# The two MLP products by seven half-block products in place of eight, sums on the vector engine

## The reference, cut to what matters

```python
h = h + mix                                   # after attention; 1024 tokens x 1024 channels
h = h + squared_relu_mlp(rms_norm(h, mlp_norm[i]), mlp_w_up[i], mlp_w_down[i])

def squared_relu_mlp(h, w_up, w_down):        # w_up 1024 x 4096, w_down 4096 x 1024
    a = jax.nn.relu(h @ w_up)
    return (a * a) @ w_down
```

## Time and profile before

| | us |
|---|---|
| median of three runs | 2296.77 |
| span of the profiled execution | 2296.6 |
| stage `so` | about 258 to 342 |
| MLP, first to last matmul | 343.15 to 1041.5 |
| final norm, first operand of the Fourier stage | to 1054 |

### The profile page before, as it was taken

How to read it: one execution, slowest core, us unless ns; L and a number is a source line. 1 busy time by engine, 2 the same in 40 slices (tenths; PEclk the granted TensorE clock), 3 DMA queues, 4 the chain that set the end, 5 groups by cost and what they waited for, 6 DMA issues and landing times.

```text
span 2296.6 us, 27818 instructions
## 1 busy us (share of the span) xinstructions
PE 2222.8 (97%) x11316; PEld 1856.7 (81%) x11316; DVE 1450.6 (63%) x2316; ACT 971.2 (42%) x1521; POOL 214.8 (9%) x316
## 2 busy tenths in 40 slices
PE   8999999999999999999999999999998999899997
PEld 6898788888888888887888898788887886688886
DVE  7777445465564555567623227378887754799996
ACT  6777422111111111134422224366766322478785
POOL 0011000011010010100000014000000100211211
PEclk9999999999999999999999999999999999899998
DMA  3123512242342343323122112000001612799996
GB/s 146 47 79 122 195 46 61 81 138 87 98 137 92 101 133 97 110 102 67 54 79 92 35 45 88 28 1 1 1 1 42 256 55 102 299 393 386 386 379 225
DMA packets 79872, 280.64 MB, mean 122 GB/s; under 512 B 9936, under 2 KB 10224, under 8 KB 78592
## 3 DMA queue, kind: packets, MB, share of 16 engines
q1 hardware_dynamic: 48960, 172.84, 21.1%
q0 software_dynamic: 29632, 101.83, 14.2%
...
HBM read 243.17 MB, written 35.66 MB: 121 GB/s over the span
## 4 chain that ended last, share of the span: by engine, by line
PE 86%; DVE 7%; ACT 4%; issue 1%; DMA 1%; POOLq 0%; SPq 0%; ACTq 0%; DVEq 0%
PE psum L98 26%; PE psum L100 25%; PE psum L99 25%; PE psum L2471 2%; PE psum L2482 2%; ACT MP_hi L2572 1%; PE psum L978 1%; DVE MP_lo L2665 1%; ACT PB L2538 1%; DVE small L2618 1%; PE psum L951 1%; PE psum L3309 1%; PE psum L3038 1%; DVE idx L3011 1%; DVE cur L3014 0%
## 5 line engine op out<-in xcount | busy, mean ns | idle before, releaser
L98 PE MATMUL psum<-U_hi,w_hi 128*128 128x512 f32 x688 | 271.0, 394 | 13.4 <-DVE w_lo L243 10.7
L234 ACT ACTIVATE w_hi<-raw 128x1024 fp32r<-128x1024 f32 (+2 forms) x163 | 162.7, 1002 | 280.5 <-PE psum L100 267.7
L99 PE MATMUL psum<-U_lo,w_hi 128*128 128x512 f32 x688 | 269.0, 391 | 0.0
L100 PE MATMUL psum<-U_hi,w_lo 128*128 128x512 f32 x688 | 268.7, 391 | 0.0
L243 DVE TENSOR_TENSOR w_lo<-raw,w_hi 128x1024 fp32r<-128x1024 f32 (+2 forms) x162 | 187.9, 1167 | 113.3 <-ACT w_hi L234 113.1
L98 PE MATMUL psum<-W_hi,w_hi 128*128 128x512 f32 x512 | 199.7, 390 | 0.9 <-DVE X L1092 0.9
L100 PE MATMUL psum<-W_hi,w_lo 128*128 128x512 f32 x512 | 199.2, 389 | 0.0
L99 PE MATMUL psum<-W_lo,w_hi 128*128 128x512 f32 x512 | 199.2, 389 | 0.0
L98 PE MATMUL psum<-a_hi,w_hi 128*128 128x512 f32 x512 | 199.2, 389 | 0.0
L99 PE MATMUL psum<-a_lo,w_hi 128*128 128x512 f32 x512 | 199.2, 389 | 0.0
L100 PE MATMUL psum<-a_hi,w_lo 128*128 128x512 f32 x512 | 199.2, 389 | 0.0
...
## 6 DMA issues: line engine op xcount, KB each, us to landing
rawe<-in_w_e SPq DMA_DIRECT2D x112, 512.0 KB, 16.9
mraw<-in_w_mod POOLq DMA_DIRECT2D x128, 256.0 KB, 3.0
rawx<-in_w_e SPq DMA_DIRECT2D x56, 512.0 KB, 18.0
raw<-in_w_up SPq DMA_DIRECT2D x32, 512.0 KB, 3.6
raw<-in_w_dn SPq DMA_DIRECT2D x32, 512.0 KB, 3.6
raw<-in_w_e SPq DMA_DIRECT2D x24, 512.0 KB, 17.0
X<-in_xT SPq DMA_DIRECT2D x8, 512.0 KB, 9.4
raw<-in_w_q SPq DMA_DIRECT2D x8, 512.0 KB, 4.9
```

What stands on the lines that cost most here:

```text
L98: e.matmul(o, l[0], r[0], start=first, stop=False, skip_group_check=skip)
L99: e.matmul(o, l[0], r[1], start=False, stop=False, skip_group_check=skip)
L100: return e.matmul(o, l[1], r[0], start=False, stop=last, skip_group_check=skip)
L234: act.e.activation(hi, src, ACT.Copy).then_inc(w_hi, 1)
```

## The change

Split both operands of a product in 2 x 2 blocks. The plain way takes eight block products; the change takes seven, with sums of blocks as operands and sums of products as results.

**First product (up).** The weight is cut into 16 groups of two column blocks (256 columns of w_up), with two halves of 512 input channels; the moving side into channel halves and token halves. Each group g is seven products of 4 x 3 matmuls, 84 in all, where two column blocks took 96. The seven moving operands B1 to B7 (four tiles of 128x512, high and low) are made once, in stage `so` and the first group, from X, in place; so X is saved to DRAM first (`x1r`) and comes back in the down stage. The form is one with few sums in which products 2, 7 and 3 are added in PSUM onto products 1, 6 and 5, after ACT has copied these out. For each group DVE makes four sums of weight halves (S1 to S4) and, from the products, the four results, their ReLU, and seven combinations t1, ..., t7 of the squared results, which SP stores to DRAM (`ta`), 256 KB each. ACT squares in place.

**Second product (down).** 7 passes of 8 steps; a step has 24 matmuls (4 output rows x 2 x 3), 1344 in all where 1536 were. A step needs three loads of 512 KB (two blocks of w_down and one of `ta`; in passes 3 and 4 of the form only one block of w_down), one DVE sum of the two blocks (passes 1, 2, 5, 6, 7), and two tiles to split. After each pass DVE adds its four results into one or two places of X (12 x 4 additions of 128x512). The weight ring has 12 raw buffers and 8 places here; splitting runs three steps ahead of PE, the sum four.

**Modulation.** 28 steps go with the groups of the up stage, 68 with steps 6 to 47 of the down stage (rows that serve both vectors are loaded once), 32 move to the later stage `gates_b`. In the first two, SP loads the rows, in the same queue as the weights.

```diff
@@ so_dve: operands of the up products, made in place
-            if 0 < n < 7:
-                u(n - 1)
-        u(6)
-        u(7)
+            if 0 < n < 5:
+                k = n - 1
+                copy_lo(dve, 1, k, X[:, k, half(0)])
+                dve.wait_ge(*so.dve("lo1", k))
+                e.tensor_tensor(X[:, k, half(0)], X[:, k, half(1)], X[:, k, half(0)], ALU.subtract).then_inc(
+                    *so.dve.one("sum5", k))
+            if 1 < n < 6:
+                copy_lo(dve, 5, n - 2, X[:, n - 2, half(0)])
+            if n > 4:
+                scaled_lo(dve, 3, n - 5, 1)
+                sum7(dve, n - 5)
+                sum6(dve, n - 5)
+        scaled_lo(dve, 3, 3, 1)
+        sum7(dve, 3)
+        for k in range(3):
+            copy_lo(dve, 7, k, X[:, k, half(1)])
         for i in range(2):
             nm2.add_half(dve, i)
-        for i in range(2):
-            nm2.inverse(dve, i)
+        copy_lo(dve, 7, 3, X[:, 3, half(1)])
+        for k in range(4):
+            scaled_lo(dve, 2, k, 0)
+        sum6(dve, 3)
@@ up_act, the head of each group
+            if g:
+                make_hi(act, T_U1[g])
+                square(g - 1, "a21", 0, "r21")
+                if g == 1:
+                    act.wait_ge(*srow_in.at(1))
+                    act.e.activation(srow[:], srow[:], ACT.Silu).then_inc(*ml.act.one("silu", 0))
+                p1(g)
+                p6(g)
+                p5(g)
@@ up_dve, one group (g > 0, not the last); up_ends(g-1) is c21, r21, lo, t6, t3, lo
+            if g:
+                up_ends(dve, g - 1)
+            else:
+                for k in range(4):
+                    copy_lo(dve, 6, k, X[:, 4 + k, half(1)])
+                make_lo(dve, T_U1[0])
...
+            if last:
+                down_sum(dve, 0)
+            else:
+                dve.wait_ge(*lo_mark(T_UY[g]))
+                weight_sums(dve, ml, g + 1)
+            if g:
+                up_last(dve, g - 1)
+            else:
+                make_lo(dve, T_U0[1])
+                for i in range(2):
+                    nm2.inverse(dve, i)
...
+            e.tensor_tensor(c[1][:], c[0][:], c[1][:], ALU.add).then_inc(*ml.dve.one("u", g))
...
+            relu(dve, c[3], bank(up_bank(g, 2)), 0, "r11", g)
...
+            e.tensor_tensor(rg[0][:], c[3][:], c[2][:], ALU.add).then_inc(*ml.dve.one("t1", g))
@@ up_pe
+        for g in range(N_G):
+            for i in THEN if g else FIRST:
+                b, (ts, h) = up_bank(g, i), OPERAND[i]
+                w = use(pe, ts[g])
+                if i in ONTO:
+                    pe.wait_ge(*ml.act(ONTO[i], g))
+                else:
+                    claim(pe, b)
+                for k in range(4):
+                    if g == 0:
+                        pe.wait_ge(*so.dve(f"lo{i}", k))
+                    m = mm3(pe.e, bank(b), cols([x[:, half(h)] for x in w], k, 128), ch(B_OP[i], k, 0, 512),
+                            k == 0 and i not in ONTO, k == 3, True)
+                m.then_inc(*ml.pe.one("u", g, i))
+                if (g, i) == (0, 5):
+                    for y in range(2):
+                        nm2.sums(pe, y)
@@ down_sp, down_dve, down_pe
+    def down_sp(sp):
+        for s in range(5, N_S):
+            down_raws(sp, s)
+            for r in down_rows(s):
+                if r > 3:
+                    sp.wait_ge(*ml.dve("mod", *row_jobs(r - 4)[-1]))
...
+                sp.e.dma_start(dmraw[r % 4][:], A["w_mod"][D_ROWS[r]]).then_inc(dmraw_in[r % 4].sem, 16)
...
+        for s in range(N_S):
+            make_lo(dve, make_ahead(s))
+            for y in evict_at(s):
+                evict(*y)
+            for r in down_rows(s):
...
+                    mod_step(dve, who, i, dmraw[r % 4], dsrow[who], to)
+            for y in squares_at(s - 1):
+                adds(*y)
+            if s + 4 < N_S:
+                down_sum(dve, s + 4)
...
+        for s in range(N_S - 2):
+            for d in range(4):
+                m = step(s, d, s % 8)
```

925 lines of the change are left out of this document (643 added, 282 removed).

## The result

The changed kernel takes 2253.43 us (median of four runs, 2251.31 to 2256.98) against 2296.36 of the kernel before on the same chip: a ratio of 0.9813, 95% interval 0.9801 to 0.9824. The prediction was 2232 with a range of 2219 to 2258. The direction was right and the time lies in the range, but the gain is 43 us where 65 were forecast. Of the 20.7 us that the spans lack, 17.7 lie in the down stage.

A forecast was written before the change was run, and what follows sets the result against it. PE was taken to bound the kernel, busy 97% of the span. Matmuls removed -87.1, up start +14.7, down stage +7, MLP end 0, gates_b modulation +0.5 sum to -64.9 from 2296.6: 2232 us, range 2219 to 2258.

The forecast's parts named there:

- The price of a matmul: In the MLP each matmul costs 0.2267 us of PE; 384 removed give -87.1 us.
- Rival 5: A matmul's price is its duration, 0.39 us, so 150 us less, 2170 us; chance 0.01.
- Steady up groups: Up groups in steady state: DVE's 17.1 us fit within PE's 19.0 per group; cost 0, hidden behind PE.
- The start: Start of the up stage: PE waits on the DVE and ACT chain to product 1's copy; +14.7 us, bounds +8 and +20.
- The down stage: Down steps: PE bounds on average, with some waits for DVE, ACT and loads; +7 us, bounds 0 and +32.
- The reserve: Down stage: DVE may fall 12.9 us behind before PE waits; steps 20 to 35 lose 14, about 2 us of waits.
- Steps 44 to 51: Down steps with additions of squares: some 13 us lost by DVE, about 0.5 us of cost.
- Steps 0 to 11: First down steps: only 2.5 us in hand, DMA also brings back X and stores; about 3 us of waits.
- Rival 1: Down stage bound by DVE or late loads by more: +10 to +30 us, 2242 to 2262; chance 0.24.
- Rival 2: Clock falls with small waits: about 6 down steps each bring a spell of 3 us, 18 us, 2250; chance 0.06.
- Rivals 3 and 4: 3: cheaper start, no down-stage waits, 2222, chance 0.16; 4: SP's modulation waits make loads late, 2420, chance 0.03.
- The end of the MLP: From last matmul through the norm's sums: 6 to 8 us against 7.3; 0, bounds -1.5 and +2.5.

The follow-up runs named there:

- the eighth product: Changed kernel with the 12 matmuls of product 4 done twice in each of the 16 up groups: 2293.7 us, ratio 0.9988 to the kernel before.
- rows later: Changed kernel with SP issuing each down-stage modulation row three iterations later, behind the weight loads of step s+3: 2247.1 us, ratio 0.9784 to the kernel before.
- short additions: Changed kernel with the 28 additions of squares for the final norm on 16 of 512 columns, part of the work left out: 2248.2 us, ratio 0.9789.
- sums first: Changed kernel with modulation rows issued three iterations later and DVE's sum of step s+4 right behind the low parts of step s+3: 2236.5 us, ratio 0.9742.
- X later: Changed kernel with X's reload spread behind down steps 2, 5, 8, 10 and first-pass results added in steps 12 to 15: 2252.3 us, ratio 0.9810.
- all: Kernel of by room, with X reloaded in pieces behind steps 2, 4, 6, 8 and first results added in steps 10 to 13: 2227.5 us, ratio 0.9698.
- by room: Kernel of three orders, with the down stage's modulation rows dealt out by DVE's load: 2234.2 us, ratio 0.9722 to the kernel before.
- three orders: Changed kernel with rows later, sums first, and the second up group's ACT copies ahead of all first-group squares, silu behind: 2233.3 us, ratio 0.9728.

## Why the prediction was right or wrong

**The price of a matmul** was right, by the eighth product in the up stage. Rival 5 (duration) is excluded.

**Steady up groups** were right: 17.1 us of DVE per group forecast, 17.15 measured (198.54 of 220 us, times 19.0), 972 matmuls per 220 us, and behind 384 us no wait of PE up to 696 us.

**The start** was right in size, +14.7 against +15.3, and in its steps: the wait ahead of the norm's sums 2.94 us (3 forecast), PE goes on behind the copy of product 1 of the second group at 383.44, 43.4 us behind the end of `so`'s last matmul (42.3 forecast), the wait there 8.48 (6 to 9 forecast), a lower clock behind it: the first matmul at 383.44 takes 0.79 us, and the silu's place in the chain is shown by its move. Of the 1.1 us too few, 0.9 is a slip of the sum: four low parts of B6 are 2.5 us at 0.62, and it went from 12.4 to 14.0 with them; DVE took 2.4 (352.84 to 355.26). Not foreseen was a third wait of 0.78 us at 361.

**The down stage** is the step that failed, +7 against +24.7. Of it 17.2 us are PE's nine waits. For 10.2 us the granted clock was at the lower level behind the two long ones, which is about 5 us at half the pace; the 2 to 3 us left were not traced. DVE's step was nearly right: 5.7 and 6.9 forecast, 5.84 and 7.04 measured (832.41 to 838.25, 863.54 to 870.58). Three sizes hung on it:
- *The reserve.* "12.9 in hand less 1 not yet regained" was not there at step 20, since SP's waits for modulation held back the loads of the passes without sums, in which it is won. The prediction named these waits but charged them only to steps with sums (1.5 us for all), and gave the steps 20 to 35 about 2 us; PE's three waits from 867 to 888 us are 4.0. Shown by rows later: 9.9 us, 1.2 of them in the two waits of the seam. My sign for it was wrong too: I looked for DVE's waits ended by DMA, of which there is nearly none from 709 us on; ACT's are the ones to look at.
- *Steps 44 to 51*, forecast 0.5. With four additions of squares in a step DVE took 8.25 us per step twice in a row (931.42 to 939.67 to 947.92), and PE's waits of 2.0 and 5.41 us and a lower clock follow. Shown by the short additions, 6.3 us of the down stage. With rows later and sums first they cost nothing, so this and the reserve are one loss seen twice, not two to be added.
- *Steps 0 to 11*, forecast 3 us, measured 5.3 of waits and the clock behind them (0.72 from 706 to 712). Here the loads were late by traffic: X's reload of 4.2 MB beside the weights. I had put "DMA has to bring back X" into the 3 us without a price. X later (3.5 us) and, within "all", 5.7 us of the stage show the size of it; that it is the reload and not the results moved along with it is read from DVE's wait of 5.02 for DMA, not shown by a run of its own.

Rival 1, DVE or late loads by 10 to 30 us, is thus what happened (17.7 above the term), and its time, 2242 to 2262, holds the measured one; its price and its mechanism were told. The range reached to 2258 for this rival's sake; that is why the time lies in it with a term off by 17.7, and no merit of the term. Its chance, 0.24, was held down by the argument that passes without sums give reserve back; that was true of DVE's work and not of the loads.

**Rival 2**, the clock with small waits. In 860 to 960 us PE paused four times by 1.3 to 2.0 us and the granted clock stayed at the upper level:

```profile
860.00:960.00 100.00, 93.58 (x406) 75.43 (x405) 84.24 (x135) 43.93 (x50) 0.54 (x1) 1.00 0.76 280
```

In the same trace it was at the lower level behind the waits of 2.94, 8.48, 4.00 and 5.41 us (0.72 in the window at 706; matmuls of 0.79 and 0.77 us at 383.44 and 980.74) and through the sums at the end of the MLP. So the rival did not come as written, one spell of 3 us behind each of some six small waits. But the length of a pause doesn't tell alone. With the rows later the clock fell behind one of 2.0 us,

```profile
699.52 0.52 PE L99 MATMUL psum<-w_hi 128*128 128x512 f32 x1 [2.04 <-DVE w_lo L281]
699.50:703.50 4.00, 3.98 (x11) 3.18 (x12) 0.00 (x0) 0.00 (x0) 0.00 (x0) 0.57 1.00 409
```

and with the short additions it stayed up behind one of 3.7 us:

```profile
709.04 0.47 PE L99 MATMUL psum<-w_hi 128*128 128x512 f32 x1 [3.67 <-DVE w_lo L281]
709.00:713.00 4.00, 3.96 (x18) 3.30 (x18) 2.87 (x3) 2.35 (x3) 0.00 (x0) 1.00 1.04 409
```

By the rule of the Trainium skill that the prediction weighed (TensorE: Matmul & The Clock Gate, "A second HAM failure mode: psum-queue depth-cycling") brief pauses between groups of matmuls would have made it swing. From 860 to 960 us this trace, as that of the experts before, does not agree for pauses up to 2.0 us; the two pauses of 2.0 us with the rows later agree with it.

**Rivals 3 and 4.** The cheaper start was not there; the down stage nearly without waits came only with the orders of "all", 22.5 us below the changed kernel's. SP's waits did make loads late, but by a few us and not by the 195 of rival 4: a load of w_dn landed in a median of 6.4 us, well under the 12 from which it would have been slower than before.

**The end of the MLP**, forecast 0, was +2.8. The changed kernel, first PE, then DVE's last result and ACT:

```profile
991.76 0.39 PE L101 MATMUL psum<-w_hi,w_lo 128*128 128x512 f32 x1
995.26 1.84 PE L1827 MATMUL psum<-vec,sq 128*128 128x2 f32 x8 [3.11 <-DVE sq L1745]
996.96 1.84 PE L1827 MATMUL psum<-vec,sqg 128*128 128x1 f32 x8
```

```profile
993.00 0.68 DVE L1736 TENSOR_TENSOR X<-X,psum 128x512 f32<-128x512 f32 x1
992.38 1.28 ACT L1715 ACT_TABLE_LOAD   x1
993.67 0.20 ACT L1715 ACTIVATE vec<-vec 128x1 f32<-128x1 f32 x1
993.78 0.61 ACT L1696 ACTIVATE sq<-X 128x512 f32<-128x512 f32 x1
```

I let both halves' sums start 2.2 us after the last matmul. They start 3.1 after its end, since two additions of the piece before (from 991.78) still stand ahead of the last result on DVE, which is taken at 993.00. The table load costs next to nothing: it ends at 993.66, when that result is ready. From the last matmul's start to the sums it is 3.50 us in place of 1.68, so 1.8 of the 2.8 us are this. For the other 1.0, all four groups of sums run at the lower level, 1.84 us each, where two of four did before (the earlier trace rows has the first, 1.02). That is not owed to the waits at 980 us: in "by room" and in "rows later, sums first" PE had no wait in the 265 us before, and all four groups still take 1.82 to 1.85 (ends of 14.8 and 15.1); in "three orders", with the same wait of 2.66 us ahead of the sums, the first two take 1.02 and 1.03, and the end is 13.0. Why the clock falls earlier in some of them stays open.

**Behind the MLP** +0.5 was forecast and +2.3 measured, within the 2.6 us by which that stretch differs among the kernels above. In it the clock was at the lower level for 50 us where it was for 39.5 before; at half the pace that is up to 5 us (an estimate), more than the whole difference. What of it belongs to the moved modulation stays open.
